# A two-layer stack in one stream of weights: the gate's last residual columns by way of DRAM, the projection's first unit inside the gate, and the gate's second half in banks 4 and 5

## The chip, the cores and the metric

The kernel runs on 1 core of one Trainium2 chip. The metric is device time in microseconds (us) of one execution. A program takes the inputs in DRAM and writes a 256 x 1024 result; everything between stays on the core but for small round trips through internal DRAM tensors.

## The reference

The sequence has 256 positions, the model 1024 columns, all in float32. Two layers of one model run, then two mixer layers of a second. Each of the first two layers is

```python
hn = rms_norm(h, norm_mix[i])
h = h + mixer(hn)                      # GLA in layer 0, differential attention in layer 1
h = h + swiglu(rms_norm(h, norm_ffn[i]), ffn_w_in[i], ffn_w_out[i])
gate = jax.nn.sigmoid(rms_norm(h, ple_norm[i]) @ ple_w_gate[i])    # 1024 x 1024
h = h + gate * (p[i] @ ple_w_proj[i])                              # 256 x 1024
```

The second model adds a short convolution mixer and a block attention (MoBA) mixer, each with a norm ahead of it. The gate step ("PLE") is where most of this change lies.

## The kernel before

All weights come as one stream of 297 units, each 128 x 1024 floats (512 KB, a 256-row by 512-column piece of a matrix), in the order in which TensorE uses them. The residual `h` (two token tiles of 128 rows) stays in SBUF for the whole run.

A float32 product is made as three float32r products. ScalarE rounds each unit to `whi` (`split_to` in its block, L671), VectorE subtracts to get `wlo` (L1079), and TensorE runs 12 matmuls a unit (L1801): 4 with `whi` and the upper half of the left side, 4 with `wlo`, 4 with `whi` and the lower half. SyncE fetches unit n into one of 4 `raw` buffers as soon as VectorE has split unit n - 4 (`fetch`, L438); `whi` and `wlo` have 8 buffers. ScalarE and VectorE split about 6 units ahead of TensorE (`AHEAD`), at places that are written out by hand between their other steps.

The left side of a product is the residual turned to columns (`x_hi`, `x_lo`, `y_hi`, `y_lo`, eight column blocks kt of 128 each). A unit of a product with 1024 rows needs two of them: unit 0 needs kt 0 and 1, unit 3 needs kt 6 and 7. There are two ways to turn the residual:

- By TensorE: `lhs_T` transposes into a PSUM bank, 4 transposes for two column blocks (L1854); ScalarE rounds them from the bank with the norm's gain (`lhs_hi`, L682), VectorE makes the lower half (`lhs_lo`, L1095).
- By a trip: VectorE transposes 32 x 32 blocks into `h_blk`, a DMA writes that to DRAM, another reads it back with the blocks moved into `h_land`; ScalarE and VectorE then make the two halves from `h_land` (L704 and L1133, in the gate L876 and L1414). Here SyncE issues both DMAs, in the order of its own queue (`second_blocks`, `gate_blocks`). Before it waits for the block it has issued the fetches up to some unit, and the later ones stand behind the trip.

The normalisation itself is a factor per token, `rstd`, made on GpSimd from sums of squares (`squares` on ScalarE, L718), and is put in when a product leaves PSUM.

The gate step of layer n is four tiles of the stream: `tple` (gate, columns 0 to 511, 4 units), `tple + 1` (projection, 1 unit), `tple + 2` (gate, columns 512 to 1023, 4 units), `tple + 3` (projection, 1 unit). In layer 0 these are units 99 to 108, in layer 1 units 207 to 216. A tile fills two PSUM banks, one for each token tile: banks 0 and 1 or banks 2 and 3 in turn. ScalarE takes the gate out by a sigmoid into `ple_gate` (L867), VectorE multiplies it with the projection's banks (`ple_gated`, L1396) and adds that to `h` (L1400). After the first half it turns columns 0 to 511 of the new residual into `h_blk` (L1404), and a trip brings them to the next mixer. After the second half, TensorE turns columns 512 to 1023 itself in layer 0 (between the first and the second unit of the next mixer), while in layer 1 they go by a trip, two pieces of two column blocks each.

The other trips of this kind, all with two pieces, lie ahead of the two first FFN tiles, of the convolution and of MoBA (`second_hi`, `second_lo`, `second_blk`). There the first eight units of two tiles are taken in the order (0,0) (0,1) (1,0) (1,1) (0,2) (0,3) (1,2) (1,3), tile and unit, so that the pieces are wanted in the fifth and sixth.

## Time and profile before

| | |
|---|---|
| median of 3 runs | 901.86 us (900.85 to 903.6) |
| profiled execution, its own time | 900.89 us |
| its span, first to last instruction | 898.7 us |
| TensorE busy | 892.9 us (99%) |
| VectorE busy | 654.6 us (73%) |
| ScalarE busy | 506.1 us (56%) |
| GpSimd busy | 63.4 us (7%) |
| granted TensorE clock | 1.000 of full speed |
| DMA | 187.47 MB, mean 209 GB/s |

A view by groups gives a busy time and the idle time before it; a timeline row gives a start in us from the start of the span, the time that the row covers, the engine, the line and the operation with its target and sources, and how many instructions were merged. Matmuls overlap, so that a row of 4 covers 1.07 us, while the next row starts 0.91 us later.

### The profile page before, as it was taken

How to read it: one execution, taken by the hardware profiler on the slowest of the kernel's cores; microseconds unless marked ns; L12 is line 12 of the kernel's file. 1: busy time of each engine (PE TensorE's matmuls, PEld its weight loads, DVE VectorE, ACT ScalarE, POOL GpSimd, SP SyncE). 2: the span in 40 equal slices, each digit the busy share in tenths (PEclk: the TensorE clock that was granted, in tenths of full speed). 3: DMA queues.
4: the chain of work that ended last, by engine and by line, in shares of the span. 5: the costliest groups of instructions: out<-in, count | busy, mean ns of one | idle time of the engine just before them, and what ended most of it. 6: DMA issues, size and time to landing. Idle time of an engine off the chain costs nothing.

```text
span 898.7 us, 12238 instructions
## 1 busy us (share of the span) xinstructions
PE 892.9 (99%) x4364; PEld 737.0 (82%) x4364; DVE 654.6 (73%) x997; ACT 506.1 (56%) x820; POOL 63.4 (7%) x75
## 2 busy tenths in 40 slices
PE   9999999999999999999999999999999999999998
PEld 8988888888888888778888888888888888887777
DVE  6985478777735699997787776646679897779764
ACT  6756555444444667688564444435664544587681
POOL 0001000000000003211100000000010000215100
PEclk9999999999999999999999999999999999999999
DMA  7674458766755655424487667746568775656621
GB/s 271 197 240 143 162 189 301 277 242 243 240 194 194 227 199 201 160 97 141 139 284 265 237 239 246 254 142 231 202 220 278 260 253 192 207 200 234 227 70 47
DMA packets 76988, 187.47 MB, mean 209 GB/s; under 512 B 6852, under 2 KB 31812, under 8 KB 76936
## 3 DMA queue, kind: packets, MB, share of 16 engines
q1 hardware_dynamic: 75480, 182.99, 59.6%
q0 software_dynamic: 1024, 3.15, 1.0%
q10 hardware_dynamic: 432, 0.66, 0.2%
q8 instruction: 31, 0.51, 0.2%
q14 instruction: 21, 0.17, 0.1%
HBM read 171.83 MB, written 14.94 MB: 208 GB/s over the span
## 4 chain that ended last, share of the span: by engine, by line
PE 95%; DMA 2%; issue 2%; DVE 1%; POOL 1%; ACT 0%; DVEq 0%; POOLq 0%
PE bank L1801 84%; PE bank L1839 3%; PE bank L1854 1%; PE bank L2114 1%; PE bank L2140 1%; DMA mb_pT<-mb_blocks 1%; DMA mb_blocks<-p_tok 1%; DMA h<-x_dram 0%; PE bank L2224 0%; PE bank L2125 0%; PE bank L2253 0%; PE bank L1961 0%; PE bank L2009 0%; PE bank L2013 0%; PE bank L2100 0%
## 5 line engine op out<-in xcount | busy, mean ns | idle before, releaser
L671 ACT ACTIVATE whi<-raw 128x1024 fp32r<-128x1024 f32 x295 | 306.2, 1060 | 186.3 <-DMA raw<-stream_dram 108.8
L1079 DVE TENSOR_TENSOR wlo<-raw,whi 128x1024 fp32r<-128x1024 f32 x295 | 347.5, 1213 | 55.6 <-ACT whi L671 54.8
L1801 PE MATMUL bank<-whi,x_hi 128*128 128x512 f32 x560 | 152.5, 394 | 0.0
L1801 PE MATMUL bank<-wlo,x_hi 128*128 128x512 f32 x560 | 149.9, 389 | 0.0
L1801 PE MATMUL bank<-whi,x_lo 128*128 128x512 f32 x560 | 149.8, 389 | 0.0
L1801 PEld LDWEIGHTS bank<-wlo,x_hi 128*128 128x128 f32 x560 | 105.1, 188 | 22.3
L1801 PEld LDWEIGHTS bank<-whi,x_lo 128*128 128x128 f32 x560 | 105.1, 188 | 22.0
L1801 PEld LDWEIGHTS bank<-whi,x_hi 128*128 128x128 f32 x560 | 103.4, 188 | 21.7 <-issue 1.2
L1801 PE MATMUL bank<-whi,y_hi 128*128 128x512 f32 x396 | 108.0, 394 | 0.1
L1801 PE MATMUL bank<-wlo,y_hi 128*128 128x512 f32 x396 | 106.0, 390 | 0.0
L1801 PE MATMUL bank<-whi,y_lo 128*128 128x512 f32 x396 | 106.0, 389 | 0.0
L1801 PEld LDWEIGHTS bank<-wlo,y_hi 128*128 128x128 f32 x396 | 74.3, 188 | 15.7
L1801 PEld LDWEIGHTS bank<-whi,y_lo 128*128 128x128 f32 x396 | 74.3, 188 | 15.7
L1801 PEld LDWEIGHTS bank<-whi,y_hi 128*128 128x128 f32 x396 | 72.8, 188 | 16.0 <-issue 0.8
L824 ACT ACTIVATE ffn_silu<-bank,rstd 128x256 f32<-128x256 f32 x44 | 18.4, 471 | 76.8 <-PE bank L1801 76.8
L1303 DVE SCALAR_TENSOR_TENSOR ffn_mid<-bank,rstd,ffn_silu 128x256 f32<-128x256 f32 x44 | 19.3, 479 | 54.0 <-ACT ffn_silu L824 54.0
L1801 PE MATMUL bank<-whi,mid_hi 128*128 128x512 f32 x176 | 47.0, 389 | 0.0
L1801 PE MATMUL bank<-wlo,mid_hi 128*128 128x512 f32 x176 | 47.0, 389 | 0.0
L1801 PE MATMUL bank<-whi,mid_lo 128*128 128x512 f32 x176 | 47.0, 389 | 0.0
L1109 DVE TENSOR_TENSOR h<-h,bank 128x512 f32<-128x512 f32 x22 | 14.1, 683 | 44.7 <-PE bank L1801 44.5
L579 POOL TENSOR_TENSOR ms<-stats 128x2 f32<-128x2 f32 x8 | 4.9, 611 | 577.1 <-ACT junk L718 577.1
L1801 PEld LDWEIGHTS bank<-wlo,mid_hi 128*128 128x128 f32 x176 | 33.0, 188 | 6.9
(251 smaller groups left out, 891.4 us busy)
## 6 DMA issues: line engine op xcount, KB each, us to landing
raw<-stream_dram SPq DMA_DIRECT2D x295, 512.0 KB, 4.6
ffn_blocks<-ffn_blk SPq DMA_DIRECT2D x22, 256.0 KB, 2.0
ffn_land<-ffn_blocks SPq DMA_DIRECT2D x22, 256.0 KB, 3.7
second_blocks<-h_blk SPq DMA_DIRECT2D x8, 256.0 KB, 2.0
h_land<-second_blocks SPq DMA_DIRECT2D x8, 256.0 KB, 3.1
cv_blocks<-cv_blk SPq DMA_DIRECT2D x7, 256.0 KB, 5.2
cv_land<-cv_blocks SPq DMA_DIRECT2D x7, 256.0 KB, 3.3
h_blocks<-h_blk SPq DMA_DIRECT2D x3, 512.0 KB, 6.3
```

Source lines behind the costliest of these rows:

```text
L579: step(nc.gpsimd.tensor_tensor(ms[:, j, 0, :], stats[:, j, 0, :], stats[:, j, 1, :], ALU.add))
L671: A(whi[:, u % RING, :], raw[:, u % RAW, :], ACT.Copy).then_inc(sem("w_hi"), 1)
L824: A(sg[:, (t - tin) % 2, k, :], bank[2 * (t % 2) + k][:, 0:256], ACT.Silu, scale=rstd[:, j, k:k + 1]).then_inc(sem("ffn_silu"), 1)
L1079: V.tensor_tensor(wlo[:, u % RING, :], raw[:, u % RAW, :], whi[:, u % RING, :].bitcast(F32), ALU.subtract).then_inc(sem("w_lo"), 1)
L1109: V.tensor_tensor(h[:, t, half * HALF:(half + 1) * HALF], h[:, t, half * HALF:(half + 1) * HALF], bank[2 * (tile % 2) + t][:, :], ALU.add) ...
L1303: V.scalar_tensor_tensor(mid[:, (t - tin) % 2, :, k, :], bank[2 * (t % 2) + k][:, 256:512].rearrange("p (k n) -> p k n", k=2), rstd[:, j, ...
L1801: last = T.matmul(bank[pair + t][:, :], lhs[a][:, kt, t * P:(t + 1) * P], w[:, u % RING, kk * NW:(kk + 1) * NW], start=part != 1 and k == ...
L1839: last = T.matmul(bank[pair + hd // 2][:, hd % 2 * SEQ:(hd % 2 + 1) * SEQ], w[:, u % RING, kk * NW + hd * P:kk * NW + (hd + 1) * P], lhs[a ...
L1854: last = T.transpose(bank[b][:, k * SEQ + t * P:k * SEQ + (t + 1) * P], src[:, t, kt * P:(kt + 1) * P], ident)
L2114: last = T.matmul(bank[DF_S_BANKS[hd][m]][:, q * SEQ:(q + 1) * SEQ], dT[r, 0, hd, q * P:(q + 1) * P], dT[r, 1, hd, :], start=True, stop=True)
L2140: last = T.matmul(bank[b][:, q * SEQ + (hd % 2) * P:q * SEQ + (hd % 2 + 1) * P], daT[:, hd % 4, k * SEQ + q * P:k * SEQ + (q + 1) * P], dv ...
```

## The change

- In the gate step, columns 768 to 1023 of the residual (kt 6 and 7) no longer go through TensorE and bank 7 but by a trip. TensorE transposes kt 4 and 5 only.
- The units of `tple` and `tple + 1` are taken in the order (0,0) (0,1) (1,0) (0,2) (0,3): the projection's unit stands third. The transposes of kt 4 and 5 stand ahead of it, one unit later than before.
- The second half of the gate (`tple + 2`) goes to banks 4 and 5. ScalarE takes the first half out after the fifth unit of the step, where it was after the fourth.
- All these trips, those of the mixers too, are issued by ScalarE and no longer by SyncE (`piece_out`, `piece_in`); SyncE's fetches have none of them between.
- In the trips' steps ScalarE's squares stand between the DMAs, one token tile at a time.

```diff
@@ order of units, names of the pieces
+PIECES = ("mix0 q0", "mix0 q1", "ple0 q1", "gate0 t0", "gate0 t1", "mix1 q0", "mix1 q1", "ple1 q1", "gate1 t0", "gate1 t1",
+          "cv q0", "cv q1", "mb q0", "mb q1")
+GATE_ORDER = ((0, 0), (0, 1), (1, 0), (0, 2), (0, 3))
@@ SyncE (second_blocks and gate_blocks are gone)
-                done = second_blocks(2 * n, tin)
                 fetch(done, done_at(tin) + 10)
                 middle(n, tin)
                 done = END[tin + FT] + 14
                 done = half_blocks(n, tin + FT)
-                done = gate_blocks(n, tin + FT + 2)
-            done = second_blocks(4, CV_IN)
+                fetch(done, END[tin + FT + 4] + 8)
+                done = END[tin + FT + 4] + 8
@@ ScalarE
+            def piece_out(name):
+
+                n = piece(name)
+                act.wait_ge(sem("g_blk"), n + 1)
+                nc.scalar.dma_start(s_dram[n], sblk[:, slot(name), :]).then_inc(sem(f"g_out{slot(name)}"), 16)
+
+            def piece_in(name):
+
+                n, q = piece(name), slot(name)
+                act.wait_ge(sem(f"g_out{q}"), 16 * turn(name))
+                nc.scalar.dma_start(sland[:, q, :, :], s_dram[n].rearrange("q n -> (q n)")
+                                    .rearrange("(i p w) -> p i w", i=P // B, p=P)).then_inc(sem(f"g_land{q}"), 16)
+            def second_hi(j, dst, name, base):
+
+                act.wait_ge(sem("h_new"), 4 * (j - 1) + 4)
+                square(j, 1, 0)
+                piece_out(f"{name} q0")
+                square(j, 1, 1)
+                piece_out(f"{name} q1")
+                piece_in(f"{name} q0")
                 split_to(base + 8)
+                piece_in(f"{name} q1")
                 for q in range(2):
...
@@ ScalarE, gate step
                 split_to(END[tple] + 1 + AHEAD)
-                lhs_hi(src, norm_gain(j), (6, 7))
-                squares(j, 1)
+                act.wait_ge(sem("h_new"), 4 * (j - 1) + 4)
+                square(j, 1, 0)
+                piece_out(f"ple{n} q1")
+                lhs_hi(src, norm_gain(j), (6,))
+                square(j, 1, 1)
+                piece_in(f"ple{n} q1")
+                split_to(END[tple] + 8)
+                pair_hi(j, src, f"ple{n} q1", 6)
                 act.wait_ge(sem("rstd"), j + 1)
                 for half in range(2):
                     t = tple + 2 * half
-                    split_to(END[t + 1] + AHEAD - 2 * half)
-                    c.wait(act, "w_used", END[t + 1])
+                    over = END[t + 1 + (half == 0)]
+                    split_to(over + AHEAD - 1 - half)
+                    c.wait(act, "w_used", over)
...
@@ VectorE, gate step
                 residual(tout + 1, 1)
+                pair_blk(f"ple{n} q1", 12 * n + 6, 6, True)
                 split_to(END[tout + 2] + 1 + AHEAD)
-                lhs_lo(src, norm_gain(j), (6, 7))
+                lhs_lo(src, norm_gain(j), (6,))
+                split_to(END[tple] + 8)
+                pair_lo(j, src, f"ple{n} q1", 6)
@@ TensorE, gate step
-                product(tple, src, "ple_sig", need=more2, hooks=[(1, second_half2)])
-                product(tple + 1, PT, "ple_gated", need=[("pT", 2 * (n + 1))])
+                for at, (t, k) in enumerate(GATE_ORDER):
+                    if at == 2:
+                        pe.wait_ge(sem("h_new"), 4 * (3 * n + 1) + 4)
+                        more2[2:3] = lhs_T(h, (6,))
+                    product(tple + t, PT if t else src, "ple_gated" if t else "ple_sig" if k == 3 else None,
+                            need=[("pT", 2 * (n + 1))] if t else more2, only=k, at=END[tple] + at)
                 half1 = []
-                product(tple + 2, src, "ple_sig")
+                product(tple + 2, src, "ple_sig", pair=4)
```

What stands on ScalarE at the start of layer 0's gate step, before (L682 rounds a bank, L718 is a square, L671 a split of a weight unit):

```order
L671 ACTIVATE whi<-raw 128x1024 [waits w_used,raw1]
L682 ACTIVATE x_hi<-bank,cols 128x256 [waits lhs_filled]
L682 ACTIVATE x_hi<-bank,cols 128x256
L682 ACTIVATE x_hi<-bank,cols 128x256 [waits lhs_filled]
L682 ACTIVATE x_hi<-bank,cols 128x256
L718 ACTIVATE junk,stats<-h 128x512 [waits stats,h_new]
L718 ACTIVATE junk,stats<-h 128x512 [waits stats]
L671 ACTIVATE whi<-raw 128x1024 [waits w_used,raw2,rstd]
```

And of the change, from the same split to the sigmoid of the gate's first half (here a split is L659, a square L729, the bank's rounding L670, the landed piece's rounding L694, the sigmoid L884):

```order
L729 ACTIVATE junk,stats<-h 128x512 [waits stats,h_new]
L680 DMA residual_blocks<-h_blk 128x512 [waits g_blk]
L670 ACTIVATE x_hi<-bank,cols 128x256 [waits lhs_filled]
L670 ACTIVATE x_hi<-bank,cols 128x256
L729 ACTIVATE junk,stats<-h 128x512 [waits stats]
L686 DMA h_land<-residual_blocks 128x4x128 [waits g_out1]
L659 ACTIVATE whi<-raw 128x1024 [waits w_used,raw2]
L694 ACTIVATE x_hi<-h_land,cols 128x256 [waits g_land1]
L694 ACTIVATE x_hi<-h_land,cols 128x256
L659 ACTIVATE whi<-raw 128x1024 [waits w_used,raw3,rstd]
L659 ACTIVATE whi<-raw 128x1024 [waits w_used,raw0]
L884 ACT_TABLE_LOAD
```

The trip out and the trip in are now ScalarE's, and two splits and the load of the sigmoid's table stand behind the wait for the piece that comes back (`g_land1`).

On ScalarE from there to the rounding of the columns that the next mixer needs first, of the change:

```order
L884 ACTIVATE ple_gate<-bank,rstd 128x512 [waits w_used]
L884 ACTIVATE ple_gate<-bank,rstd 128x512
L659 ACTIVATE whi<-raw 128x1024 [waits w_used,raw1]
L659 ACTIVATE whi<-raw 128x1024 [waits w_used,raw2]
L680 DMA residual_blocks<-h_blk 128x512 [waits g_blk] x2
L729 ACTIVATE junk,stats<-h 128x512 [waits stats]
L686 DMA h_land<-residual_blocks 128x4x128 [waits g_out0]
L729 ACTIVATE junk,stats<-h 128x512 [waits stats]
L686 DMA h_land<-residual_blocks 128x4x128 [waits g_out1]
L659 ACTIVATE whi<-raw 128x1024 [waits w_used,raw3]
L899 ACTIVATE y_hi<-h_land,cols 128x128 [waits g_land0]
```

Before, the four DMAs of this place stood on SyncE, and a split, both squares and the rounding (L876) followed each other here with no DMA between.

On TensorE, from the projection's unit (`p_hi`) to the gate's last unit of the first half, of the change (L1837 is the product's line there; the transposes of kt 4 and 5 stand just ahead):

```order
L1837 MATMUL bank<-whi,p_hi 128x512 [waits pT,w_hi,h_new]
L1837 MATMUL bank<-whi,p_hi 128x512 x3
L1837 MATMUL bank<-wlo,p_hi 128x512 [waits w_lo]
L1837 MATMUL bank<-wlo,p_hi 128x512 x3
L1837 MATMUL bank<-whi,p_lo 128x512 x4
L1837 MATMUL bank<-whi,x_hi 128x512 [waits w_hi,lhs_hi]
L1837 MATMUL bank<-whi,x_hi 128x512 x3
L1837 MATMUL bank<-wlo,x_hi 128x512 [waits w_lo]
L1837 MATMUL bank<-wlo,x_hi 128x512 x3
L1837 MATMUL bank<-whi,x_lo 128x512 [waits lhs]
L1837 MATMUL bank<-whi,x_lo 128x512 x3
L1837 MATMUL bank<-whi,x_hi 128x512 [waits w_hi,g_hi]
```

Before, both units of kt 4 to 7 waited for `lhs_hi` (a rounded bank); the last one now waits for `g_hi`, the piece that comes back from DRAM, and the projection's unit stands ahead of both.

## Rows read from the trace of the kernel before

**Rows 1.** The page's first part: busy time, share of the span, instructions

```profile
span 898.7 us, 12238 instructions
PE 892.9 (99%) x4364; PEld 737.0 (82%) x4364; DVE 654.6 (73%) x997; ACT 506.1 (56%) x820; POOL 63.4 (7%) x75
```

**Rows 2.** A wait of TensorE, the latest in the program: total, times, longest

```profile
PE bank L2253 <- DMA mb_pT<-mb_blocks: 1.1, 2, 0.7
```

**Rows 3.** Timeline of TensorE, gate step of layer 0 and next mixer's start

```profile
299.50 1.07 PE L1801 MATMUL bank<-whi,x_hi 128*128 128x512 f32 x4
...
302.23 1.03 PE L1854 MATMUL bank<-consts,h 128*128 128x128 f32 x8
303.02 1.17 PE L1801 MATMUL bank<-whi,x_hi 128*128 128x512 f32 x4
...
327.61 1.16 PE L1801 MATMUL bank<-whi,y_hi 128*128 128x512 f32 x4
...
330.44 1.06 PE L1854 MATMUL bank<-consts,h 128*128 128x128 f32 x8
```

**Rows 4.** Timeline of ScalarE in the same stretch

```profile
302.87 1.57 ACT L682 ACTIVATE x_hi<-bank,cols 128x256 fp32r<-128x256 f32 x4 [0.51 <-PE bank L1854]
304.30 0.65 ACT L718 ACTIVATE junk<-h 128x512 f32<-128x512 f32 x1
...
305.07 0.63 ACT L718 ACTIVATE junk<-h 128x512 f32<-128x512 f32 x1
...
307.15 2.96 ACT L671 ACTIVATE whi<-raw 128x1024 fp32r<-128x1024 f32 x3 [1.36 <-POOL rstd L574]
310.13 1.28 ACT L867 ACT_TABLE_LOAD   x1
...
325.08 1.28 ACT L876 ACTIVATE y_hi<-h_land,cols 128x128 fp32r<-128x128 f32 x4 [1.48 <-DMA h_land<-gate_blocks]
326.26 1.24 ACT L867 ACTIVATE ple_gate<-bank,rstd 128x512 f32<-128x512 f32 x2
```

**Rows 5.** Timeline of VectorE in the same stretch

```profile
299.70 1.28 DVE L1109 TENSOR_TENSOR h<-h,bank 128x512 f32<-128x512 f32 x2 [2.73 <-PE bank L1801]
...
314.27 1.28 DVE L1396 TENSOR_TENSOR ple_gated<-ple_gate,bank 128x512 f32<-128x512 f32 x2 [3.66 <-PE bank L1801]
...
317.89 1.10 DVE L1404 STREAM_TRANSPOSE h_blk<-h 128x512 f32<-128x512 f32 x1
...
327.87 1.28 DVE L1396 TENSOR_TENSOR ple_gated<-ple_gate,bank 128x512 f32<-128x512 f32 x2 [0.86 <-PE bank L1801]
329.07 1.28 DVE L1400 TENSOR_TENSOR h<-h,ple_gated 128x512 f32<-128x512 f32 x2
```

**Rows 6.** Timeline of SyncE's queue in the same stretch (DMA issues)

```profile
317.31 2.04 SPq L512 DMA_DIRECT2D gate_blocks<-h_blk  x2
319.39 2.09 SPq L515 DMA_DIRECT2D h_land<-gate_blocks  x2
321.83 26.74 SPq L451 DMA_DIRECT2D raw<-stream_dram  x13
```

**Rows 7.** Timeline of layer 1's end and the convolution's start, several engines

```profile
654.68 2.22 DVE L1119 STREAM_TRANSPOSE h_blk<-h 128x256 f32<-128x256 f32 x4
660.57 0.91 ACT L704 ACTIVATE x_hi<-h_land,cols 128x256 fp32r<-128x256 f32 x2 [2.13 <-DMA h_land<-second_blocks]
662.88 1.07 PE L1801 MATMUL bank<-whi,x_hi 128*128 128x512 f32 x4
```

**Rows 8.** The tile `h_land`: time from a DMA's issue to its landing

```profile
DMA to landing us min/median/max: 2.6/3.2/4.9
```

**Rows 9.** Timeline of ScalarE's queue at the kernel's start

```profile
0.73 0.44 ACTq L741 DMA_DIRECT2D raw<-stream_dram  x1
```

**Rows 10.** Timeline of the first FFN's start: a second piece, and its user

```profile
129.97 0.91 ACT L704 ACTIVATE x_hi<-h_land,cols 128x256 fp32r<-128x256 f32 x2 [1.64 <-DMA h_land<-second_blocks]
133.58 1.07 PE L1801 MATMUL bank<-whi,x_hi 128*128 128x512 f32 x4
```

More of the change, by code:

```diff
@@ L76, with piece, slot, turn @@
 LAST = ((0, 0, NW), (1, 0, NW // 2), (1, NW // 2, NW))
+PIECES = ("mix0 q0", "mix0 q1", "ple0 q1", "gate0 t0", "gate0 t1", "mix1 q0", "mix1 q1", "ple1 q1", "gate1 t0", "gate1 t1",
+          "cv q0", "cv q1", "mb q0", "mb q1")
+GATE_ORDER = ((0, 0), (0, 1), (1, 0), (0, 2), (0, 3))
 PAIR_ORDER = ((0, 0), (0, 1), (1, 0), (1, 1), (0, 2), (0, 3), (1, 2), (1, 3))
+def piece(name):
+    return PIECES.index(name)
+def slot(name):
+    return int(name[-1])
+def turn(name):
+    return sum(slot(other) == slot(name) for other in PIECES[:piece(name) + 1])
 def done_at(tile):
@@ L686, in norm_gain, with pair_hi @@
                 return lambda kt: cols[:, C_NORM + j * KT + kt:C_NORM + j * KT + kt + 1]
+            def piece_out(name):
[7 more added lines that the diff above has]
+                                    .rearrange("(i p w) -> p i w", i=P // B, p=P)).then_inc(sem(f"g_land{q}"), 16)
+            def pair_hi(j, dst, name, kt0):
+                q = slot(name)
+                act.wait_ge(sem(f"g_land{q}"), 16 * turn(name))
+                for k in range(2):
+                    A(dst[0][:, kt0 + k, :].rearrange("p (t i b) -> p t i b", t=TT, b=B),
+                      sland[:, q, :, :].rearrange("p i (k t b) -> p k t i b", k=2, t=TT)[:, k], ACT.Copy,
+                      scale=norm_gain(j)(kt0 + k)).then_inc(sem("g_hi"), 1)
             def mixer_lhs(j, dst, out):
@@ L1123, in second_lo, with pair_blk @@
-            def second_lo(j, dst, r, base):
+            def pair_blk(name, news, kt0, first):
+                for t in range(TT):
+                    if first:
+                        dve.wait_ge(sem("h_new"), news + t + 1)
+                    at = slice(kt0 * P, (kt0 + 2) * P)
+                    last = V.transpose(sblk[:, slot(name), :].rearrange("p (f k t b) -> p t f k b", f=P // B, k=2, t=TT)[:, t],
+                                       h[:, t, at].rearrange("p (k b f) -> p f k b", b=B, f=P // B))
+                last.then_inc(sem("g_blk"), 1)
@@ new lines, in pair_lo @@
+            def pair_lo(j, dst, name, kt0):
+                n = piece(name)
+                for k in range(2):
+                    kt = kt0 + k
+                    dve.wait_ge(sem("g_hi"), 2 * n + k + 1)
+                    for t in range(TT):
+                        at = slice(t * P, (t + 1) * P)
+                        part = sland[:, slot(name), :, :].rearrange("p i (k t b) -> p k t i b", k=2, t=TT)[:, k, t]
+                        last = V.scalar_tensor_tensor(dst[1][:, kt, at].rearrange("p (i b) -> p i b", b=B), part,
+                                                      norm_gain(j)(kt),
+                                                      dst[0][:, kt, at].bitcast(F32).rearrange("p (i b) -> p i b", b=B),
+                                                      ALU.mult, ALU.subtract)
+                last.then_inc(sem("g_lhs"), 1)
@@ L1137, in second_lo @@
-                    last.then_inc(sem("g_lhs"), 1)
-                dve.wait_ge(sem("g_lhs"), 2 * (r + 1))
+                    pair_lo(j, dst, f"{name} q{q}", 4 + 2 * q)
+                dve.wait_ge(sem("g_lhs"), piece(f"{name} q1") + 1)
             def parts_out(out, j, dst):
@@ L1859, in lhs_T, with piece_need, second_need @@
                 return need
-            def second_need(r):
-                return [("g_lhs", 2 * r + q + 1, ("g_hi", 4 * r + 2 * q + 2)) for q in range(2)]
+            def piece_need(name):
+                return ("g_lhs", piece(name) + 1, ("g_hi", 2 * piece(name) + 2))
+            def second_need(name):
+                return [piece_need(f"{name} q{q}") for q in range(2)]
             def first_tiles(tile, lhs, signal, need, beside=None):
```

121 lines of the change are left out of this document (40 added, 81 removed).

## The prediction

> **What bounds the kernel now.** I read the page's first part first: TensorE is busy 892.9 of 898.7 us [rows 1]. Whatever moves the time must do it through TensorE: fewer instructions there, or a new wait. Then its waits: they are small, and the one shown, by the attention of the last mixer, is 1.1 us in all [rows 2]; none lies in the gate steps. So nothing is to be won by bringing an operand earlier. What can be won is what TensorE no longer does, and what can be lost is any operand that now comes later than its unit. Third, the timelines of the engines over the gate step of layer 0, for how much room each operand has. A weight unit takes 302.23 - 299.50 = 2.73 us, and the eight transposes behind it 303.02 - 302.23 = 0.79 us [rows 3]. The reader is to see one tight place: VectorE ends the residual's second half at 329.07 + 1.28 = 330.35 [rows 5], and TensorE starts its transposes of it at 330.44 [rows 3]. There is 0.09 us of room. Layer 1's gate step runs 324.40 us later in the same rhythm.
>
> **What goes.** Four of eight transposes per gate step, 0.79 / 2 = 0.40 us, twice: 0.8 us. That is all of TensorE's work that the change takes away; the order of units and the other banks change no instruction's length.
>
> **The first new trip (kt 6 and 7), layer 0.** VectorE ends the residual at 300.98 [rows 5] and turns two blocks of 0.55 us (2.22 / 4) [rows 7]: done at 302.1. ScalarE was free at 302.87 - 0.51 = 302.36 [rows 4]. A square takes 0.77 us (304.30 to 305.07) [rows 4], so the DMA out is issued at 303.1 and lands some 2 us later (from 317.31 to 319.39, at which SyncE could issue the way back [rows 6]). That is hidden, since ScalarE waits for TensorE next: the transposes now stand behind two units, at 299.50 + 5.46 = 304.96; the bank is full 0.64 us later (302.23 to 302.87), at 305.6. Two roundings at 0.36 (four from 302.87 to 304.30) and a square bring the DMA in to 307.1. From issue to landing such a DMA took 2.6 to 4.9 us, median 3.2 [rows 8]. The short ones ran while SyncE held back its weight loads: its next load follows the trip, at 321.83 [rows 6]. Now SyncE holds nothing back, and three loads of 512 KB are let go at 303 to 306 as VectorE splits. I take 3.6 us, between median and maximum. The piece lands at 310.7, and two roundings (0.91 us [rows 7]) end at 311.6. TensorE wants it at 304.96 + 0.40 + 2 x 2.73 = 310.8. It waits 0.8 us; at 2.6 us not at all.
>
> **The sigmoid.** Behind that piece in ScalarE's queue stand two splits (2.96 / 3 = 0.98 each), the table load (1.28) and the two sigmoids (1.24) [rows 4]: 311.6 + 1.96 + 1.3 + 1.24 = 316.1. VectorE's multiplication started at 314.27 [rows 5], when TensorE's projection ended; it now waits for ScalarE and is 1.8 us late. Its two blocks were done 3.04 us (317.31) and 4.72 us (317.89 + 1.10 = 318.99) behind that start, now at 319.1 and 320.8. An issue on ScalarE's queue took 0.44 us [rows 9] (bounds of what it holds up: nothing, if the arithmetic runs on beside it, to 0.44 each); I take the whole. DMA out t1 at 320.8, square, DMA in t0 at 322.0, square, DMA in t1 at 323.2. Before, the last was issued at 319.39 + 2.09 - 0.38 = 321.1. At 3.6 us it lands at 326.8 (before 325.08 [rows 4]). Four roundings (1.18) and two sigmoids (1.24) end at 329.3. Before, VectorE's second multiplication started at 327.87, bound by TensorE [rows 5]. It needs 2.48 us to the new residual: 331.8, where it was 330.35.
>
> **Where TensorE pays, layer 0.** The transposes of that residual were at 330.44 and are now at 331.8: +1.35 us. This is the whole sum of the layer, with the 0.40 us won and the 0.8 us of the first wait inside it, since both only change how long TensorE stands at this place. The first unit of the next mixer itself wants a rounding of t1 at about 327.5 against 328.0 on TensorE, and isn't late. The second gate half being in banks 4 and 5 is what keeps the late second sigmoid from holding up that unit too; it costs nothing.
>
> **Layer 1.** The same up to the second sigmoid, which ends at 329.3 + 324.4 = 653.7. Then four splits (3.92) and a square: DMA out q0 at 658.4; with an issue, a square and another issue, and 2 us for landing, the DMA in of q0 at 660.4. It took 2.7 us before; I take 3.4: 663.8, and rounded at 664.7. TensorE's unit stood at 662.88 [rows 7]: +1.8 us. The piece q1 comes a split later, about 666.4, for a unit at 667.4, so it adds nothing.
>
> **The mixers' trips.** The second piece at the first FFN was rounded at 129.97 + 0.91 = 130.88 for a unit at 133.58 [rows 10], 2.7 us of room. On ScalarE's queue it is later by a split and a square, at most 1.8 us. Hidden there, at layer 1's FFN and at MoBA; the cover gone, each costs what exceeds 2.7.
>
> **Weights.** SyncE isn't held up by blocks any more, but nothing on TensorE waited for a load. ScalarE stands in waits for DMAs for some 2 to 3 us at a time while it is four units, 10.9 us, ahead. Nothing.
>
> **The sum.** 1.35 + 1.8 = 3.15 us. The profiled execution took 900.89 us, so 904.0; its time lies 0.97 under the median of the runs shown, so for a median 905.0.
>
> **A rule against it.** In the Trainium skill, "DMA: Bandwidth & Descriptors", section "Issuing engines are not separate DMA queues", DMAs of all issuers run on the same 16 engines and interleave, and another issuer saves only issue time. By the Trainium skill again, same page, "Queues, rings and completion order", an engine takes turns between queues packet by packet, so a trip on ScalarE's queue would share with weight loads what it had alone on SyncE's. The rows agree as far as they go: trips took 2.6 us at best and 4.9 at most. By the clean rows alone the sum would be -0.8 us, by full sharing it goes to the third case below.
>
> **The rivals.** (a) *Clean trips, not slower.* If a way in takes 2.7 us even beside loads and an issue holds ScalarE up for nothing, the first piece is rounded at 310.7, VectorE's first multiplication starts at 315.2, t1 comes back at 324.9 and TensorE finds the residual at 330.0 when it wants it. At the convolution q0 is rounded at 337.6 + 324.4 = 662.0. Only the transposes count: 905.0 - 3.15 - 0.8 = 901.1, no change that can be told. It decides where a way in takes under about 2.8 us. For it: the median of 3.2 has both kinds; against it: loads run in these stretches. (b) *Trips in full contention.* With 4.9 us for each way in, the first residual is ready at 334.3 (+3.9) and q0 at 668.8 (+5.9): 905.0 - 3.15 + 9.8 = 911.7; with 4.3 us about 908. Against it: 4.9 is the maximum of all. The rule that the Trainium skill states ("DMA: Bandwidth & Descriptors", "Queues, rings and completion order") would act in this way. (c) *ScalarE becomes the bound* by its 28 issues (12 us at 0.44) and TensorE waits for `whi`: against it its 56% [rows 1]. It would need ScalarE four units behind; 908 and up. (d) *Faster by more than 0.3%* needs 2.7 us, and TensorE has only 0.8 less to do; no row gives the rest.
>
> **How the numbers follow.** About 0.3% (2.7 us) is what a measurement of this kernel can tell from no change. The forecast, a late chain in both gate steps (+1.5 to +5 us), 0.60; (a) 0.22; (b) 0.12; (c) 0.02; (d) 0.04. In the forecast's case about 0.34 of the 0.60 lies over 2.7 us, for 3.15 is close to it; with (b) and (c) slower is 0.48, with (a) and the forecast's lower part the same is 0.48, faster 0.04. The likeliest case alone spans 903.4 to 906.9. The range goes down to (a), 900.9, and up to 908.0, which leaves the worst half of (b) and (c) out.
>
> **What the profile of the changed kernel would show.** Right: x4 for the transposes in the gate steps; TensorE idle ahead of the gate's fourth unit (0 to 2 us, its releaser the rounding of the landed piece), ahead of the transposes at the start of the second mixer (about 1 us, by VectorE's addition), and ahead of the convolution's fifth unit (about 1.4 us); the second sigmoid ending 1 to 2 us behind TensorE's projection; ways in of 3 to 4 us. Wrong: no idle at these places (a), or idle by `whi` (c), or idle at an FFN's or MoBA's fifth unit, which I hold for hidden.

## The result and the profile after

The changed kernel takes 913.82 us (median of 5 runs, 912.48 to 915.58) where the kernel before, on the same chip, takes 901.05 us (5 runs, 900.67 to 903.6): a ratio of 1.014, 95% interval 1.0125 to 1.0155. That is 12.8 us slower. Forecast was 905.0 with a range of 900.9 to 908.0: the direction was right, the size lies outside the range, beyond even the rival of full contention (911.7). The profiled execution took 913.59 us at a granted clock of 1.000.

The page's first part for the kernel after, to be read beside [rows 1]:

```profile
PE 893.6 (98%) x4356; PEld 735.5 (81%) x4356; DVE 658.4 (72%) x1005; ACT 505.3 (55%) x820; POOL 65.3 (7%) x75
```

TensorE is busy for 893.6 us and was for 892.9, although it has eight transposes fewer; the span has grown by 911.8 - 898.7 = 13.1 us. So nearly the whole loss is waiting. The view of waits, TensorE's lines only (total, times, longest in us), says for what; of these only `mb_pT` stood in [rows 2], with 1.1 us:

```profile
PE bank L1837 <- ACT x_hi L694: 5.7, 3, 2.1
PE bank L1837 <- ACT y_hi L899: 1.7, 1, 1.7
...
PE bank L2293 <- DMA mb_pT<-mb_blocks: 1.6, 1, 1.6
PE bank L1837 <- ACT y_hi L694: 1.4, 1, 1.4
PE bank L1837 <- ACT x_hi L899: 1.3, 1, 1.3
...
PE bank L1890 <- DVE h L1436: 1.1, 1, 1.1
```

L694 and L899 are ScalarE's roundings of a landed piece (`pair_hi`, and the loop over the gate's t0 and t1). Five groups, 11.2 us, are new, and the four of ScalarE's are all behind a trip. The timeline of TensorE shows their places (start, time covered; in brackets the idle time before and its releaser), to be read beside [rows 3] and [rows 7]:

```profile
304.65 0.60 PE L1890 MATMUL bank<-consts,h 128*128 128x128 f32 x4
305.01 1.18 PE L1837 MATMUL bank<-whi,p_hi 128*128 128x512 f32 x4
...
309.68 1.07 PE L1837 MATMUL bank<-whi,x_lo 128*128 128x512 f32 x4
...
312.63 1.21 PE L1837 MATMUL bank<-whi,x_hi 128*128 128x512 f32 x4 [1.89 <-ACT x_hi L694]
...
330.96 1.16 PE L1837 MATMUL bank<-whi,y_hi 128*128 128x512 f32 x4 [1.67 <-ACT y_hi L899]
...
335.01 1.09 PE L1890 MATMUL bank<-consts,h 128*128 128x128 f32 x8 [1.08 <-DVE h L1436]
...
641.76 1.20 PE L1837 MATMUL bank<-whi,y_hi 128*128 128x512 f32 x4 [1.45 <-ACT y_hi L694]
...
659.71 1.15 PE L1837 MATMUL bank<-whi,x_hi 128*128 128x512 f32 x4 [1.33 <-ACT x_hi L899]
...
672.54 1.20 PE L1837 MATMUL bank<-whi,x_hi 128*128 128x512 f32 x4 [1.71 <-ACT x_hi L694]
...
677.69 0.50 PE L1837 MATMUL bank<-whi,x_hi 128*128 128x512 f32 x1 [2.13 <-ACT x_hi L694]
```

The four transposes hold TensorE for 305.01 - 304.65 = 0.36 us. Then it stands at the gate's fourth unit (312.63 and 641.76), at the first unit of the next mixer (330.96) and of the convolution (659.71), at the transposes in layer 0 (335.01), and at the fifth and sixth units of the convolution (672.54, 677.69). A wait costs a little more than its bracket, for the group that follows is longer too. Counted from where a group would have started, 0.91 us behind the one before it, the seven delays are 2.04, 1.83, 1.24, 1.60, 1.49, 1.87 and 2.29 us, 12.4 in all, in the order of the rows. Less 0.8 for the transposes and with 0.5 for `mb_pT` (1.6 us against 1.1 before) that is 12.1 of the 13.1 us.

The cause of the waits stands in ScalarE's timeline of layer 0 (ACTq is its DMA queue), to be read beside [rows 4]:

```profile
305.29 0.47 ACT L670 ACTIVATE x_hi<-bank,cols 128x256 fp32r<-128x256 f32 x1 [3.41 <-PE bank L1890]
305.30 0.37 ACTq L686 DMA_DIRECT2D h_land<-residual_blocks  x1
...
311.68 0.91 ACT L694 ACTIVATE x_hi<-h_land,cols 128x256 fp32r<-128x256 f32 x2 [3.99 <-DMA h_land<-residual_blocks]
...
323.96 0.38 ACTq L686 DMA_DIRECT2D h_land<-residual_blocks  x1
...
330.01 1.28 ACT L899 ACTIVATE y_hi<-h_land,cols 128x128 fp32r<-128x128 f32 x4 [3.34 <-DMA h_land<-residual_blocks]
```

The chain of work that ended last (start, time) runs in this stretch through both ways in, up to the residual that VectorE ends at 334.95 and the transposes at 335.01 wait for:

```profile
305.30 6.35 DMA h_land<-residual_blocks
...
321.82 2.12 DMA residual_blocks<-h_blk
323.96 6.03 DMA h_land<-residual_blocks
```

The way in of the new trip leaves at 305.30 and ends at 311.65, 6.35 us later; that of the gate's t1 leaves at 323.96 and ends 6.03 us later. The page's DMA issues have all fourteen trips; the tile `h_land` has two DMAs more, each of 512 KB and issued by SyncE, and is to be read beside [rows 8]:

```profile
residual_blocks<-h_blk ACTq DMA_DIRECT2D x14, 256.0 KB, 2.1
...
h_land<-residual_blocks ACTq DMA_DIRECT2D x14, 256.0 KB, 5.7
```

```profile
DMA to landing us min/median/max: 2.8/5.3/8.8
```

The way out still takes 2.1 us. The way in has now a median of 5.7 us, and takes 8.8 at most (the convolution's q1). Of the twelve trips before, issue by issue, the median was 2.9 us and the longest 4.3. The DMA view shows what runs beside the way in of 305.30 (q1 is SyncE's queue of weight loads, q10 ScalarE's; packets, MB, share of the 16 engines). First 307 to 309 us, then 309 to 311.7:

```profile
q1 hardware_dynamic: 158, 0.57, 86.7%
q10 hardware_dynamic: 67, 0.03, 5.7%
```

```profile
q1 hardware_dynamic: 178, 0.65, 65.3%
q10 hardware_dynamic: 461, 0.23, 28.1%
```

The loads go in packets of some 3.6 KB (0.57 MB / 158), the piece in packets of 0.5 KB. Between 307 and 309 us the piece got 67 packets, 5.7% of the engines' time, and the loads 86.7%. It moved for good only behind 309. Of the three loads that were under way when it was issued, one had landed at 307.01, one at 308.69. From 305 to 307 it moved nothing. Some 1 us of that is not the loads' doing: in r1 below, with no load in flight, the first packet of the same piece moves 1.04 us behind its issue. In the change it moves 2.8 us behind it.

### The profile page after: what moved, and what is told of

It reads as the page before. It is cut to its first block, busy times and chain, and to the rows that moved or that the text cites. A ratio compares the mean times of both kernels' runs of the same rounds, so it can differ in the third digit from the quotient of the medians.

```text
span 911.8 us, 12232 instructions
## 1 busy us (share of the span) xinstructions
PE 893.6 (98%) x4356; PEld 735.5 (81%) x4356; DVE 658.4 (72%) x1005; ACT 505.3 (55%) x820; POOL 65.3 (7%) x75
## 3 DMA queue, kind: packets, MB, share of 16 engines
q0 software_dynamic: 1024, 3.15, 1.0%
## 4 chain that ended last, share of the span: by engine, by line
PE 81%; DVE 7%; DMA 7%; ACT 3%; issue 2%; POOL 1%; ACTq 0%; DVEq 0%; SPq 0%; POOLq 0%
PE bank L1837 71%; DMA h_land<-residual_blocks 4%; PE bank L1875 3%; DVE wlo L1103 2%; ACT whi L659 1%; PE bank L1890 1%; DMA residual_blocks<-h_blk 1%; PE bank L2180 1%; DMA mb_pT<-mb_blocks 1%; PE bank L2154 1%; PE bank L2264 1%; PE bank L2293 1%; DVE h_blk L1440 0%; DVE df_m L1520 0%; DVE df_tok L1524 0%
## 5 line engine op out<-in xcount | busy, mean ns | idle before, releaser
L659 ACT ACTIVATE whi<-raw 128x1024 fp32r<-128x1024 f32 x295 | 305.6, 1059 | 195.5 <-DMA raw<-stream_dram 123.2
L1837 PE MATMUL bank<-whi,x_hi 128*128 128x512 f32 x560 | 153.1, 395 | 7.2 <-ACT x_hi L694 5.7
L1837 PE MATMUL bank<-wlo,x_hi 128*128 128x512 f32 x560 | 150.0, 390 | 0.0
L1837 PE MATMUL bank<-whi,x_lo 128*128 128x512 f32 x560 | 149.8, 389 | 0.0
L1837 PEld LDWEIGHTS bank<-whi,x_hi 128*128 128x128 f32 x560 | 103.1, 188 | 30.8 <-ACT x_hi L694 7.6
L1837 PEld LDWEIGHTS bank<-wlo,x_hi 128*128 128x128 f32 x560 | 105.2, 188 | 22.3
L1837 PEld LDWEIGHTS bank<-whi,x_lo 128*128 128x128 f32 x560 | 105.1, 188 | 22.0
L1837 PE MATMUL bank<-whi,y_hi 128*128 128x512 f32 x396 | 108.1, 395 | 3.4 <-ACT y_hi L899 1.7
L1837 PE MATMUL bank<-wlo,y_hi 128*128 128x512 f32 x396 | 106.1, 390 | 0.0
L1837 PE MATMUL bank<-whi,y_lo 128*128 128x512 f32 x396 | 106.0, 390 | 0.0
L1837 PEld LDWEIGHTS bank<-whi,y_hi 128*128 128x128 f32 x396 | 72.8, 188 | 20.0 <-issue 3.2
L1837 PEld LDWEIGHTS bank<-wlo,y_hi 128*128 128x128 f32 x396 | 74.3, 188 | 15.7
L1837 PEld LDWEIGHTS bank<-whi,y_lo 128*128 128x128 f32 x396 | 74.3, 188 | 15.7
L1837 PE MATMUL bank<-wlo,mid_hi 128*128 128x512 f32 x176 | 47.0, 389 | 0.0
L1837 PE MATMUL bank<-whi,mid_hi 128*128 128x512 f32 x176 | 47.0, 389 | 0.0
L1837 PE MATMUL bank<-whi,mid_lo 128*128 128x512 f32 x176 | 47.0, 389 | 0.0
L1837 PEld LDWEIGHTS bank<-whi,mid_lo 128*128 128x128 f32 x176 | 33.0, 188 | 6.9
```

Source lines behind the costliest of these rows:

```text
L659: A(whi[:, u % RING, :], raw[:, u % RAW, :], ACT.Copy).then_inc(sem("w_hi"), 1)
L1837: last = T.matmul(bank[pair + t][:, :], lhs[a][:, kt, t * P:(t + 1) * P], w[:, u % RING, kk * NW:(kk + 1) * NW], start=part != 1 and k == ...
```

## The experiments

**Theory A**: the way in is slow because it now lies in another queue than the weight loads while these run: on SyncE's queue the later loads stood behind it, now they take turns with it, and its small packets get little in a turn. **Theory B**: DMAs on ScalarE's queue are slow, or late, of themselves. **Theory C**: the order of units, the late sigmoid and the transposes' new place cost most. Each kernel was compared with the kernel before on the same chip, which took 901.06 us (r1 to r4), 901.44 (r5 to r8) and 901.48 (r9).

### r1: ScalarE issues, the loads are held back until the piece has landed

SyncE calls this at the old trips' places, and at the new one's:

```diff
+            def trip(names, at):
+                fetch(done, at)
+                for name in names:
+                    sp.wait_ge(sem(f"g_land{slot(name)}"), 16 * turn(name))
+                return max(done, at)
...
+                done = trip((f"ple{n} q1",), END[tin + FT + 2] + 8)
+                done = trip((f"gate{n} t0", f"gate{n} t1"), END[tin + FT + 4] + 8)
```

> The changed kernel, ScalarE still issues all 14 trips, but SyncE stops its weight loads at each trip until its pieces have landed (it stops at the units at which the kernel before stopped, and at the eighth unit of the gate step for the new trip). Theory A, the ways in are slow because they share the DMA engines with weight loads in flight: they fall from a median of 5.7 us to 3.2 or less, TensorE's 11.2 us of waits for landed pieces and for the residual shrink to under 3, and the time is 900 to 904 us. Theory B, a DMA that ScalarE's queue issues is slow by itself: the ways in stay at 5 us and more, the time stays at 912 to 915. Theory C, ScalarE's blocked order (DMA waits, squares, splits ahead of the sigmoid) is what makes operands late whatever a trip takes: ways in fall, but TensorE's waits keep over half their size, 907 or more.

Measured: 907.22 us, ratio 1.0069 (1.005 to 1.0089). The tile `h_land`; its longest, 4.1 us, is one of SyncE's two of 512 KB, and the fourteen ways in, still on ScalarE's queue, took 2.54 to 3.09 us:

```profile
DMA to landing us min/median/max: 2.5/2.8/4.1
```

Theory B falls: the queue is as fast as SyncE's when nothing runs beside it. The wait at the gate's fourth unit is gone in both layers. But the time is not what A was to give: 900 to 904 us and under 3 us of waits for pieces and residual were expected, and 907.22 lies where C was to lie (907 or more). The waits speak against C as well: those behind landed pieces and the residual, 11.2 us in the change, are down to 2.1 (1.1 at the convolution's fifth unit, 1.0 at the transposes), with the 2.5 shown below to 4.6, less than half. So 6 us over the kernel before are left, and most of their cause is new. Its largest waits of TensorE, and a row of ScalarE's timeline just ahead of the first:

```profile
PE bank L1847 <- ACT y_hi L680: 2.5, 1, 2.5
PE bank L2303 <- DMA mb_pT<-mb_blocks: 1.7, 1, 1.7
```

```profile
333.29 1.06 ACT L669 ACTIVATE whi<-raw 128x1024 fp32r<-128x1024 f32 x1 [2.39 <-DMA raw<-stream_dram]
```

ScalarE stands for a late weight load, does its splits late, and the roundings behind them reach TensorE 2.48 us late at the second mixer. Here the first load behind the trip goes out at 326.64, where the kernel before had sent it at 321.83. The matmuls behind this wait are slow as well (last section). So holding the loads until the landing takes more from the stream than it can give at this place.

### r2: SyncE issues all fourteen trips

Only the queue goes back, and with it the hold of the later loads behind each trip; the new trip, the order, the banks and the late sigmoid stay. The same helper issues both DMAs, in SyncE's queue, and ScalarE's `piece_out` and `piece_in` do nothing:

```diff
+                for name in names:
+                    sp.wait_ge(sem("g_blk"), piece(name) + 1)
+                    sp.dma_start(s_dram[piece(name)], sblk[:, slot(name), :]).then_inc(sem(f"g_out{slot(name)}"), 16)
+                for name in names:
+                    q = slot(name)
+                    sp.wait_ge(sem(f"g_out{q}"), 16 * turn(name))
+                    sp.dma_start(sland[:, q, :, :], s_dram[piece(name)].rearrange("q n -> (q n)")
```

> The changed kernel with all trips, the new one too, issued by SyncE in its own queue, with the weight loads behind them, as the kernel before did; the order of units, the banks, the new trip and the late sigmoid stay. Theory A (sharing with loads): ways in at 2.7 to 4, time 900 to 903 us, within 0.3% of the kernel before. Theory B (ScalarE's queue slow by itself): the same, so this run doesn't part A and B. Theory C (the gate step's new order): waits of 1 to 2 us at the transposes and at the convolution remain, 904 or more.

Measured: 902.15 us (10 runs), ratio 1.0012 (1.0 to 1.0024); `h_land` 2.6/2.8/4.4 us, the fourteen trips at most 3.9. So 11.7 of the 12.8 us hang on which queue issues, with all that this does to the loads and to ScalarE, which no longer stands in waits for the trips; some 1 us (by the interval 0 to 2.2) is left for all the rest. Theory C falls for the main part.

### r3: the kernel before, with only the queue moved to ScalarE

Twelve pieces, the old order, eight transposes, banks 0 to 3; `piece_out` and `piece_in` stand in ScalarE's block as in the change:

```diff
-PIECES = ("mix0 q0", "mix0 q1", "ple0 q1", "gate0 t0", "gate0 t1", "mix1 q0", "mix1 q1", "ple1 q1", "gate1 t0", "gate1 t1",
+PIECES = ("mix0 q0", "mix0 q1", "gate0 t0", "gate0 t1", "mix1 q0", "mix1 q1", "gate1 t0", "gate1 t1",
...
-                product(tple + 2, src, "ple_sig", pair=4)
+                product(tple + 2, src, "ple_sig")
```

> The kernel before with nothing but the queue moved: its 12 pieces are issued by ScalarE in the changed kernel's places and SyncE holds no load; the gate step has its old order, banks and eight transposes. Theory A: ways in of 5 to 6 us beside loads, waits at the start of the second mixer, at the transposes there and at the convolution, together 5 to 9 us: 906 to 910 us. If the new gate order is what costs, this run stays within 0.3% of the kernel before.

Measured: 909.27 us, ratio 1.0078 (1.0049 to 1.0107); `h_land` 2.8/4.8/7.3. The queue alone, without the new trip, costs some 7 to 8 us (by the interval 4 to 10). Its largest wait isn't for a piece itself:

```profile
PE bank L1825 <- ACT ple_gate L875: 5.8, 2, 3.2
```

ScalarE waits for the slow t1 and so takes out the second gate half late; that half lies in banks 0 and 1, which the next mixer's first unit wants. Banks 4 and 5 take this wait for a bank away, as the prediction said of them. Without them the waits at that unit are 2.61 and 3.22 us where the change has 1.67 and 1.33; t1's way in took 6.67 and 7.30 us in this run against 6.03 and 5.65, so the difference isn't the banks' alone. The second of these waits does more. Rows of TensorE's timeline behind it, and the windows (length, busy us of PE, PEld, DVE, ACT and POOL with instructions, then the granted clock, the DMA share and GB/s):

```profile
657.52 2.05 PE L1825 MATMUL bank<-whi,x_hi 128*128 128x512 f32 x4 [3.22 <-ACT ple_gate L875]
659.36 1.91 PE L1825 MATMUL bank<-wlo,x_hi 128*128 128x512 f32 x4
...
664.07 1.07 PE L1825 MATMUL bank<-wlo,x_hi 128*128 128x512 f32 x4
```

```profile
652.00:656.00 4.00, 2.29 (x11) 1.56 (x9) 0.28 (x2) 1.01 (x4) 0.00 (x0) 1.00 0.76 291
656.00:660.00 4.00, 2.48 (x6) 2.04 (x7) 3.47 (x9) 4.00 (x6) 0.00 (x0) 0.59 0.02 6
660.00:664.00 4.00, 4.00 (x11) 3.11 (x11) 4.00 (x6) 2.54 (x6) 1.35 (x1) 0.55 0.35 131
```

The granted clock falls from 1.00 to the lower of its two levels (1.2 GHz): over 656.8 to 663.5 us it reads 0.50, and the last two windows hold a rest at 1.00. It falls while TensorE still waits. The groups of four stand some 1.7 us apart instead of 0.91. From 657.52 to 664.07 there are four steps in 6.55 us instead of 3.64: 2.9 us more.

### r4 and r8: the way in with larger and with smaller rows

r4 reads a piece in rows of 2 KB, r8 in rows of 256 bytes, where the change has 512. Both leave out the right order of the blocks, so the numbers that are computed change; bytes, DMAs and waits stay.

```diff
# r4
-                nc.scalar.dma_start(sland[:, q, :, :], s_dram[n].rearrange("q n -> (q n)")
-                                    .rearrange("(i p w) -> p i w", i=P // B, p=P)).then_inc(sem(f"g_land{q}"), 16)
+                nc.scalar.dma_start(sland[:, q, :, :].rearrange("p i n -> p (i n)"), s_dram[n])\
+                    .then_inc(sem(f"g_land{q}"), 16)
# r8
+                nc.scalar.dma_start(sland[:, q, :, :].rearrange("p i (c w) -> p (i c) w", c=2),
+                                    s_dram[n].rearrange("q n -> (q n)")
+                                    .rearrange("(i p w) -> p i w", i=2 * P // B, p=P)).then_inc(sem(f"g_land{q}"), 16)
```

> The changed kernel, but a way in reads its piece back as it was written, one row of 2 KB per partition instead of four of 512 bytes, so that the blocks are not moved to their places (this part of the computation is changed). Same bytes, same queue, same moment. Theory A1, the engines take turns packet by packet, so that a piece in 512-byte packets gets a ninth of the time beside loads in 4 KB packets: a piece in 2 KB packets gets a third, the ways in fall to 3 to 4 us and the time to 902 to 907. Theory A2, the bytes are shared evenly or the loads ahead are simply served first: the ways in stay at 5 to 6 us, 911 to 915.

> The changed kernel with the way in cut into rows of 256 bytes instead of 512 (the blocks then land in the wrong places: this part of the computation is changed). With 2 KB rows the median of the tile's ways in fell from 5.3 to 4.3 us and the shortest from 2.8 to 2.7. If a piece's share beside loads follows the size of its packets, the ways in beside loads grow clearly, to 6.5 us and more, and the time to 916 or more, while the shortest grow by under 1 us. If the size of packets doesn't matter beside loads, both grow alike or not at all and the time stays within 2 us of the changed kernel.

| way in | time, us | ratio (95%) | `h_land` min/median/max, us |
|---|---|---|---|
| 2 KB rows (r4) | 911.75 | 1.0109 (1.0081 to 1.0137) | 2.7/4.3/6.6 |
| 512 bytes (the change) | 913.82 | 1.014 (1.0125 to 1.0155) | 2.8/5.3/8.8 |
| 256 bytes (r8) | 923.58 | 1.0274 (1.0239 to 1.0308) | 3.2/5.3/9.3 |

The time and the longest way in grow as the rows shrink, as A says, but the median of r8 stayed at 5.3 where I expected 6.5 or more, and r4's time is far from the 902 to 907 that turns by packets were to give. The longest ways in grow most: the gate's t1 in layer 0 leaves at 323.55 and takes 8.7 us where the change took 6.0, and TensorE pays for it:

```profile
PE bank L1838 <- ACT x_hi L695: 5.3, 3, 2.2
PE bank L1838 <- ACT x_hi L900: 5.0, 1, 5.0
PE bank L1838 <- ACT y_hi L900: 4.4, 1, 4.4
```

Not all of this is the DMA's. With the same 4356 matmuls TensorE was busy for 893.6 us in the change's profiled execution, and in r8's for:

```profile
PE 899.1 (98%) x4356; PEld 740.2 (80%) x4356; DVE 657.9 (72%) x1005; ACT 505.7 (55%) x820; POOL 67.2 (7%) x75
```

So 5.5 of the 8.3 us between these two spans are slower matmuls, at a granted clock of 0.50 around the waits of 4.45, 5.01 and 1.88 us, and only the other 3 are more waiting. In r4 the clock hides a gain: its two executions at full clock took 909.39 and 910.38 us, the change's two 913.59 and 913.82, some 4 us more, while the medians differ by 2. Small packets make it worse, but are not needed for most of the 12.8 us.

### r5: the change without the new trip

kt 6 and 7 go through TensorE and bank 7 again; ScalarE's queue, the order of units and banks 4 and 5 stay.

```diff
-                pair_hi(j, src, f"ple{n} q1", 6)
...
-                        more2[2:3] = lhs_T(h, (6,))
+                        more2[2:4] = lhs_T(h, (6, 7))
```

> The changed kernel without its new trip: columns 768 to 1023 of the residual go through TensorE and bank 7 again, with the transposes of kt 4 to 7 ahead of the projection's unit; ScalarE still issues the other 12 pieces beside loads, the order of units, banks 4 and 5 and the late sigmoid stay. The moved queue alone cost about 8 us and the whole change 12.8, everything without the queue 1. If the rest is the new trip on the slow way (TensorE's two waits of 1.9 and 1.5 us for it, and the chain that it delays), this run gives 907 to 910. If the late sigmoid and the order are what make the difference, it stays at 912 or more.

Measured: 909.02 us, ratio 1.0094 (1.0075 to 1.0113); `h_land` 2.9/4.7/6.6. The new trip in the slow way is worth the difference of the ratios, 0.0046 or some 4 us (with both intervals, 2 to 6); by r2 it costs nearly nothing on SyncE's queue.

### r6: as r1, but the loads are held only until the piece is in DRAM

```diff
-                    sp.wait_ge(sem(f"g_land{slot(name)}"), 16 * turn(name))
+                    sp.wait_ge(sem(f"g_out{slot(name)}"), 16 * turn(name))
```

The loads are then let go at the moment at which the way in is issued. This is what stood in the kernel before and in r2, except that there both lay in one queue, the way in first.

> The changed kernel, ScalarE issues all trips, and SyncE stops its loads at each trip only until the pieces have landed in DRAM, that is until the moment at which ScalarE issues the way in. So loads and way in start together, from two queues; in the kernel before they start together from one queue, the way in first. If what counts is only how many loads are already under way, the ways in take 3 to 3.5 us and the time is 901 to 905. If a way in on a queue of its own loses against loads that start with it, they take 4 us and more and the time is 905 to 911.

Measured: 918.3 us, ratio 1.017 (1.0147 to 1.0193), slower than the change itself and than the 905 to 911 expected. TensorE's busy time is up by 5.0 us here too (898.6), at a mean granted clock of 0.994. r2 holds its loads to the same moment and took 902.15 us. The first FFN's second piece tells most. Of r6, ScalarE's timeline, and TensorE's:

```profile
125.34 0.40 ACTq L696 DMA_DIRECT2D h_land<-residual_blocks  x1
...
134.73 0.91 ACT L704 ACTIVATE x_hi<-h_land,cols 128x256 fp32r<-128x256 f32 x2 [6.72 <-DMA h_land<-residual_blocks]
```

```profile
135.69 1.19 PE L1847 MATMUL bank<-whi,x_hi 128*128 128x512 f32 x4 [2.23 <-ACT x_hi L704]
```

The DMA view of r6 from 125.3 to 133 us, and of the kernel before from 125.6 to 130 us, when the same piece went in (issues, KB each, median us to landing):

```profile
raw<-stream_dram SPq DMA_DIRECT2D x4, 512.0 KB, 6.7
h_land<-residual_blocks ACTq DMA_DIRECT2D x1, 256.0 KB, 9.4
```

```profile
raw<-stream_dram SPq DMA_DIRECT2D x4, 512.0 KB, 6.3
h_land<-second_blocks SPq DMA_DIRECT2D x1, 256.0 KB, 4.3
```

Both times one piece and four loads, issued within two microseconds. In one queue, the piece ahead of the loads, it takes 4.3 us. In a queue beside theirs it takes 9.4 us, while the loads take about what they took. The first piece of the same pair, issued 1.05 us ahead of these loads, took 2.7 us in r6. One thing besides the queue differs: the piece was issued 0.04 us ahead of the first load in r6, 0.42 us in the kernel before. It doesn't explain the loss: the gate's t1 in layer 0 of r6 had 0.37 us of lead and no load in flight and took 6.26 us, where pieces with 0.41 to 0.42 us in SyncE's queue took 2.7 to 4.4 in the kernel before, r2, r7 and r9. The other second pieces of r6 took 9.00, 4.36, 8.02 and 8.57 us, against 3.42, 2.91, 3.69 and 3.50 before. This is theory A, shown in the DMA's own time, with C out of play.

### r7: SyncE issues; only order, late sigmoid and banks 4 and 5 of the change

r2's helper and r5's edit together, eight transposes, no new trip.

> Only the order of units in the gate step, the later sigmoid and banks 4 and 5; SyncE issues the 12 old pieces and holds its loads as before, and kt 6 and 7 go through TensorE. Eight transposes a step stay, so nothing is won on TensorE. If the late sigmoid (a unit later, a table load and two splits ahead of it) makes the residual late at the transposes of the second mixer, where there was 0.09 us of room, the time is 902 to 904; if it is hidden, 901 to 902.

Measured: 902.41 us (12 runs), ratio 1.0015 (1.0002 to 1.0028). One wait of TensorE is due to it, in layer 0 at 331.60:

```profile
PE bank L1892 <- DVE h L1438: 1.0, 1, 1.0
```

The first half of the gate is taken out a unit later, so VectorE starts it at 315.42 where it was 314.27 and ends the residual later than TensorE wants it. The chain that ended last there also has t0's way in, 4.84 us where the kernel before took 2.90, with no load in flight at its issue in either; so how much of the 1.0 us is the order's isn't shown.

### r9: SyncE issues; new trip and banks 4 and 5, but the old order

r2's helper, and the units and the sigmoid as they were, to see whether what is left of the change is of use:

```diff
-                    over = END[t + 1 + (half == 0)]
-                    split_to(over + AHEAD - 1 - half)
+                    over = END[t + 1]
+                    split_to(over + AHEAD - 2 * half)
...
-                for at, (t, k) in enumerate(GATE_ORDER):
...
+                product(tple, src, "ple_sig", need=more2, hooks=[(1, turn_pair)])
+                product(tple + 1, PT, "ple_gated", need=[("pT", 2 * (n + 1))])
```

> The new trip for kt 6 and 7 and banks 4 and 5 alone: SyncE issues every piece in its queue and holds its loads as before, the gate's four units come before the projection's and the sigmoid follows the fourth, as before. The piece should be rounded at about 307.9 us of the span for a unit at 308.1, so both gate steps save 0.4 us of transposes with no new wait. If the late sigmoid was what cost the version with the new order its 1 us, this one is 0.5 to 0.9 us faster than the kernel before (900.5 to 901); if the trip itself costs, TensorE waits at the fourth unit and nothing is won.

Measured: 902.84 us (12 runs), ratio 1.0014 (1.0004 to 1.0024): the expected 0.5 to 0.9 us faster missed. In layer 0 the gate's fourth unit doesn't wait, in layer 1 it does:

```profile
PE bank L1844 <- ACT y_hi L702: 1.5, 1, 1.5
```

There the way out was issued at 625.97 and took 3.9 us, and the way in landed at 632.72. A trip of two DMAs has to fit between the residual and the fourth unit, and this way out takes the room. At this place it took 3.5 to 3.9 us in every kernel that has it, on either queue, with a load in flight and without (r6), against 2.0 to 2.2 us in layer 0; why isn't known. r2 has it too (3.8 us), and with the new order, a unit more of room, TensorE doesn't wait there. No kernel here beats the one before.

## Why the prediction was right and wrong

**The step that failed: "I take 3.6 us, between median and maximum"** for a way in on ScalarE's queue beside loads. The bounds were 2.6 and 4.9 us from [rows 8], and the upper one was no bound. Every one of those DMAs stood in SyncE's queue, the twelve trips ahead of the loads that they met. And the 4.9 us are not a trip's, for the tile has DMAs of two sizes:

```profile
h_land<-second_blocks SPq DMA_DIRECT2D x8, 256.0 KB, 3.1
h_land<-h_blocks SPq DMA_DIRECT2D x2, 512.0 KB, 4.6
h_land<-gate_blocks SPq DMA_DIRECT2D x4, 256.0 KB, 2.9
```

4.88 us is the longer of the two of 512 KB; the trips took 2.57 to 4.31 us. Measured are 6.35 (new trip, layer 0), 6.03 (gate's t1), 5.70 and 5.65 in layer 1, 4.7 and 8.8 at the convolution. r1, r2 and r6 show what it is: a median of 2.8 us with loads held, 2.8 in SyncE's queue, 9.4 against 4.3 for the same piece beside loads of another queue. The prediction's own rival (b) had this mechanism but priced it from the same rows (4.9 us) and gave it 0.12; the price was too low, and 0.12 was little for what came. The reason stood in the text: "SyncE holds nothing back". I used it to choose a value inside the range, where it took the range away.

Of the rule weighed there: by the Trainium skill, "DMA: Bandwidth & Descriptors", "Queues, rings and completion order", an engine goes round the queues packet by packet. The direction agrees: a queue of 0.5 KB packets loses beside one of 3.6 KB packets (5.7% against 86.7% from 307 to 309 us). At 256 bytes the longest ways in are longer (9.3 us against 8.8), the median is not. Turns of one packet each, as the profile counts packets, are not what the counts show: 67 against 158, then 461 against 178. Whether these are the packets that the Trainium skill means no run here shows. By the Trainium skill, same page, "Issuing engines are not separate DMA queues", another issuer saves only issue time and its DMAs interleave. Here the measurement differs in weight: they interleave, but against one queue's order that costs a small urgent DMA 5 us (9.4 against 4.3).

**The new trip in layer 0**, forecast 0.8 us of wait at the gate's fourth unit: 1.89 measured, and 1.45 in layer 1. The place is right. The way in left at 305.30 instead of the forecast 307.1, since the issue doesn't stand behind roundings and a square in time; that won 1.8 us back, and the way in itself lost 2.75 against the 3.6 taken.

**The first mixer unit behind the gate**, "isn't late": wrong, 1.67 us at 330.96 and 1.33 at the convolution's first unit. t1 was rounded by about 331 and not 327.5.

**The transposes**, forecast 1.35 us as the whole sum of layer 0. The mechanism is right: TensorE starts them when the residual is ready, and the waits ahead lie inside that. The size is not: the transposes start at 335.01 where they started at 330.44, 4.57 us later, since VectorE's second multiplication starts at 332.47, not at 329.3. That the wait there is 1.08 us, near to 1.35, is chance, for TensorE had by then stood at two places before.

**The convolution**, forecast 1.8 us at its fifth unit: 1.71 measured, and the agreement is luck. That unit stood at 662.88 and stands at 672.54, with most of the delay from waits before it, and q0's way in left at 666.85 instead of 660.4 and took 4.7 us instead of 3.4. "The piece q1 ... adds nothing": wrong, 2.13 us at 677.69, after a way in of 8.8 us.

**The gain**, 0.8 us for eight transposes fewer: right, four take 0.36 us in layer 0 where eight took 0.79. **The mixers' trips and the weights**: right, no FFN, no MoBA unit waits for a piece, nor TensorE for a load. **ScalarE as the bound** (rival c): no, it is busy for 505.3 us and no unit of TensorE waits for `whi`. **Banks 4 and 5**: right, by r3, where the same unit waits 2.61 and 3.22 us for the bank. **An issue held to cost ScalarE 0.44 us**: no, as the last section has it.

**The sum**: 3.15 us forecast, 13.1 measured by span. The queue alone makes 7 to 8 (r3), the new trip on it some 4 (the change and r5), the order and the late sigmoid 1 (r7). These are differences of runs with intervals of 1 to 3 us each way, and r3's has waits for a bank and a fall of the clock in it that the change's profiled execution hasn't; that they add up to the whole is no proof of each.

**What stays open**: some 1 us of the 13.1; by what rule the engines share between two queues; why r8's median way in did not rise; and why the way out at layer 1's gate takes near 4 us.

## What to carry to other kernels

In this kernel a small DMA on the path belonged into the queue that carries the bulk loads, ahead of those that were not urgent yet: its place in that queue was its protection (a way in took at most 4.8 us there in all these kernels), and a queue of its own took this away as soon as both ran at once (up to 9.4 us). A landing time read from a trace holds for the size, the queue and the neighbours that it had; when a change takes away what held the neighbours back, the old maximum is no upper bound. If such a DMA must be issued elsewhere, make its rows long (some 4 us of the 12.8 here, from 512 bytes to 2 KB) and look at whether the stream can bear being held, since too much of that starves it (r1).

## What was not expected of the hardware

- The same 256 KB took 4.3 us ahead of four 512 KB loads in their queue and 9.4 us beside them from another queue (r6 and before).
- DMA issues of ScalarE cost its arithmetic nothing that shows: issue at 305.30 for 0.37 us, rounding from 305.29 to 305.76 beside it. The 0.44 us of [rows 9] that the prediction counted for each was not paid.
- Around waits of 1.8 to 5.0 us TensorE's granted clock fell in some executions to 0.50. In r3 this cost 2.9 us behind a wait of 3.22 us. In r1 the four matmuls behind the wait of 2.48 us took 2.08 us instead of some 1.2. r4 has it at a wait of 2.14 us, the profiled execution of the change has nothing of it at one of 2.13, though three of the change's five executions show a mean of 0.998. Why one wait does it and another doesn't stays open. A kernel that makes TensorE wait can so lose more than the wait.
